# A two-model transformer block on one core: shared SBUF tiles moved to addresses that are multiples of 128 bytes

## The chip, the core and the metric

The kernel runs on 1 core of a Trainium2 chip, as one launch. The metric is the device time of that launch in microseconds (us), the median of several runs. Names of engines: PE is TensorE (matmul), PEld its weight loads, DVE VectorE, ACT ScalarE, POOL GpSimd, SP the queue that starts most DMAs. SBUF is the on-chip memory; addresses in this document are byte offsets within one of its 128 partitions. A fp32r matmul reads fp32 words in one pass; a plain fp32 matmul is split into several.

## What is computed

The reference is a chain of two models on one sequence of 512 tokens and 1024 features, all in fp32. Cut to what matters here:

```python
# first model, two layers
for layer in range(2):
    x = x + 0.5 * swiglu_ffn(rms_norm(x, ...), w_gu[layer], w_down[layer])   # 1024 -> 2 x 2816 -> 1024
    h = rms_norm(x, ...)
    x = x + (even_mixer if layer == 0 else odd_mixer)(h, ...)                # banded, stick-breaking, dilated attention
    x = x + memory_cross_attention(rms_norm(x, ...), rms_norm(mem, ...), ...)# 256 memory rows, 4 heads of 256
    x = x + 0.5 * swiglu_ffn(rms_norm(x, ...), ...)
# second model, one layer
proj = rms_norm(x, ...) @ w_in
y_a = (rg_lru(conv(xr), ...) * gelu(gr)) @ w_rnn_out
y_b = dsa_sparse_attention(q, k, v, iq, ik, iw) @ w_att_out                  # top 128 of the keys per query
mix = (sigmoid(g_a) * y_a + sigmoid(g_b) * y_b) @ w_o
x = x + rms_norm(mix, ...)
f = (silu(h @ w_gate) * (h @ w_up)) @ w_down
x = x + rms_norm(f, ...)

def swiglu_ffn(x, w_gu, w_down):
    gate, up = split(x @ w_gu, 2)
    return (silu(gate) * up) @ w_down
```

## The kernel before

**Big products.** Nearly all the work is a fixed list of products with weights (`gemm_table`), run one after the other by `pe_products`. Activations stand transposed, features on the partitions: a tile `[128, K, 512]` holds K slices of 128 features by 512 tokens (2048 bytes a slice). Precision comes from splitting: each operand is held as an upper part and a remainder, both of type fp32r, and a product is three matmuls, upper by upper, upper by remainder, remainder by upper. The loop runs over column groups of the weight; in a group over chunks of two K slices; over the slice; over up to four output banks; and over the three products. With K slices and four banks a group has K x 4 x 3 matmuls: 96 where K is 8, 264 where K is 22.

**Two forms.** In form A the weights are the stationary operand (128 x 128) and the activations stream past (moving operand, 512 columns). In form B it is the other way round: the activations are stationary, the weights move. In the names of the profile, `ps<-hTh,wh` is written moving operand first.

**Weights.** The SP queue brings weight chunks from HBM into four buffers `raw`; ACT copies each to `wh` (upper part), DVE computes `wl = raw - wh`. Four buffers each, prepared up to three chunks ahead (`act_split`, `dve_split`).

**Activations.** Five kinds of tiles feed the big products:
- `hTh`, `hTl`: the normalised input of most products, with an SBUF place of their own;
- `f..Fh`, `f..Fl` (class `Ffn`): the gated product of a feed-forward, 22 slices, read by the down projection; four times in form A (`f1d0`, `f2d0`, `f1d1`, `f2d1`), the last time in form B (`f3d`);
- `c0mh`, `c0ml` (class `Cross`, and `c1..`): the normalised memory, read by the key and value projection of the cross attention, form B, 4 groups of 48 matmuls per layer;
- `s_Yh`, `s_Yl`: the recurrence's output, form A, 2 groups (within `ya`);
- `s_Zh`, `s_Zl`: the merged branches, form A, 2 groups (`wo`).

**Where tiles lie.** The weights' buffers, `xT` and `hTh`/`hTl` have fixed places below `base`. All other tiles share the space above it and are laid out anew for each stage, by class `Area`: a running offset `at`, and `take`, which gives a tile the offset and steps on by its size rounded up to 32 bytes (lines 148 to 161). `sb` without an area allocates from the fixed part, in the order of the calls (lines 271 to 290). `base` is the end of the fixed part rounded up to 64 (line 296). Small tiles taken in between (one column of 4 bytes, 8 statistics) move what follows by 32 bytes.

```python
    def take(self, nc, name, shape, dt):
        n = 4 * int(np.prod(shape[1:]))
        t = nc.alloc_sbuf_tensor_at(name, shape, dt, offset=self.at)
        self.at += -(-n // 32) * 32
        return t
```

**Attention.** Scores, transposes and value products of the three attention stages are plain fp32 matmuls on tiles of those areas (`o_kT`, `s_kT`, `e_kbT`, `..PT`), mixed by `pe_stage` with the matmuls of the neighbouring big products. The order of everything is written out by hand; there is no scheduler.

**Start.** `x_rows` (the input), `prm` (parameters) and `misc` (identity matrix, masks) are loaded, PE transposes the input, ACT and DVE split it into `hTh` and `hTl`. At the end PE runs `f3d`, then ACT, POOL and DVE scale by the norm and SP stores.

Of the kernel before, what the change touches and what calls it, by code (L numbers as in the profile page):

```python
# [13 lines left out]
P = 128  # L14
# [133 lines left out]
class Area:  # L148
# [4 lines left out]

    def take(self, nc, name, shape, dt):
        n = 4 * int(np.prod(shape[1:]))
        t = nc.alloc_sbuf_tensor_at(name, shape, dt, offset=self.at)
        self.at += -(-n // 32) * 32
        return t
# [13 lines left out]
def params_layout():  # L172
    names = []
    for l in range(2):
        names += [(f"ffn1_norm{l}", 8), (f"mix_norm{l}", 8), (f"xa_norm{l}", 8), (f"xa_mem_norm{l}", 8),
                  (f"ffn2_norm{l}", 8), (f"xa_q_gain{l}", 2), (f"xa_k_gain{l}", 2)]
    names += [("ev_q_gain", 1), ("ev_k_gain", 1), ("od_q_gain", 1), ("od_k_gain", 1), ("ev_sinks", 8),
              ("norm_mix_pre", 8), ("norm_mix_post", 8), ("norm_ffn_pre", 8), ("conv_b", 8), ("rg_b_a", 8), ("rg_b_x", 8),
              ("rg_lambda", 8), ("conv_w", 32)]
    at, off = {}, 0  # L180
    for n, w in names:
        at[n] = (off, w)
        off += w
    return at, off


PRM, NPRM = params_layout()
# [71 lines left out]
def program(nc, T, out):  # L259
    ctx = ExitStack()  # L260

    def sb(name, shape, dt=F32, area=None):
        if area is None:
            return ctx.enter_context(nc.sbuf_tensor(name, shape, dt))
        return area.take(nc, name, shape, dt)
# [12 lines left out]
    wl = [sb(f"wl{i}", [P, 2, 512], F32R) for i in range(NW)]  # L278
    xn_at = nc.sbuf_base
    xn = [sb(f"xn{i}", [P, D]) for i in range(2)]  # L280
    prm = sb("prm", [P, NPRM])
    misc = sb("misc", [P, NMISC])
    half = sb("half", [P, 64])
    stat = sb("stat", [P, 16])
    ones = sb("ones", [P, P])
    rc = sb("rc", [P, 8])
    coef = sb("coef", [P, 8])
    la = sb("la", [P, 5, 8])
# [4 lines left out]
    def rate(t):  # L293
        return rc[:, 4 + t:5 + t]

    base = -(-nc.sbuf_base // 64) * 64

    def par(name):
        o, w = PRM[name]
# [1163 lines left out]
    ev = Area(base)  # L1463
# [10 lines left out]
    ev_gone = ev.sub()  # L1474
    e_ta = sb("e_ta", [P, NT, 512], F32, ev)
    e_kd = sb("e_kd", [P, NT, 256], F32, ev)
    ev.at += 64
    e_R = sb("e_R", [P, S], F32, ev)
    ev_xn = Area(xn_at)
    ev_q = Area(xn_at + 2048)  # L1480
# [1268 lines left out]
```

How the kernel before makes its waits and increments, by code:

```python
    def wait_ge(self, flag, key):  # L75
        if self.e is None:
            return
        sem, value, who, place = flag.at[key]
        if who is not None:
            if self.seen.get(who, 0) >= place:
                return
            self.seen[who] = place
        else:
            if self.seen.get(sem, 0) >= value:
                return
            self.seen[sem] = value
        self.e.wait_ge(sem, value)
# [272 lines left out]
    def handover(e, key):  # L360
        e.last.also(ended, (key, e.name)) if e.last.place else e.last.then_inc(ended, (key, e.name))
        if e.name != "pe":
            for who in ("pe", "act", "dve", "pool"):
                e.wait_ge(ended, (key, who))
# [2 lines left out]
    def sp_weights(sp):  # L368
        for n, (segs, kp) in enumerate(stream):
            r, o = n % NRAW, 0
            if n >= NRAW:
                sp.wait_ge(w_hi, n - NRAW)
                sp.wait_ge(w_lo, n - NRAW)
            for w, c, width, _, _ in segs:
                sp.dma_start(raw[r][:, :, o:o + width], w[kp * 256:(kp + 1) * 256, c:c + width].rearrange(
                    "(c p) n -> p c n", p=P)).then_inc(raw_in[r], n, 16)
                o += width
# [1 line left out]
    def act_split(act, upto):  # L379
        while act.split <= min(upto, len(stream) - 1):
            n = act.split
            W = chunk(n)
            act.wait_ge(raw_in[n % NRAW], n)
            if n >= NW:
                act.wait_ge(w_used, n - NW)
            act.activation(wh[n % NW][:, :, 0:W], raw[n % NRAW][:, :, 0:W], AF.Copy).then_inc(w_hi, n)
```

## Time and profile before

| | us |
|---|---|
| median of 3 runs | 3221.99 (3221.38 to 3222.6) |
| the profiled execution, its own time | 3222.08 |
| its span, first to last instruction | 3220.4 |
| PE busy | 3143.0 (98% of the span) |
| DVE busy | 1573.0 (49%) |
| ACT busy | 1223.4 (38%) |
| POOL busy | 345.3 (11%) |
| HBM traffic | 286.42 MB read, 90 GB/s over the span |

The span and the profiled execution's own time differ by 1.7 us, which lies outside the instructions. Busy is the union of an engine's instructions; a matmul of the trace begins when the one before it is still draining, so for the rate of PE one reads the distance between the starts of two matmuls (below: the interval), not the duration of one (about 0.39 us here). The mean granted TensorE clock is 0.991 of full speed.

### The profile page before, as it was taken

To read this page: it belongs to the slowest core of one execution; us is meant where nothing else is said; L and a number is where in the kernel's file an instruction comes from. 1 tells how busy PE (TensorE), PEld (TensorE's weight loads), DVE (VectorE), ACT (ScalarE), POOL (GpSimd) and SP (SyncE) were. 2 spreads that over 40 slices of the span, in tenths; PEclk is the share of its full clock that TensorE was granted. 3 is DMA by queue.
4 is the path that set the end of the run, shared out by engine and by line. 5 is a ranking of instruction groups with operands and counts; after the bars stand their busy time and mean duration, and the time that the engine had idled before them with its cause. 6 is when DMAs were issued, how large, how long until landed. Compare 5 with 4: busy or idle time off the path is not lost.

```text
span 3220.4 us, 36941 instructions
## 1 busy us (share of the span) xinstructions
PE 3143.0 (98%) x14404; PEld 2517.4 (78%) x14404; DVE 1573.0 (49%) x2425; ACT 1223.4 (38%) x2008; POOL 345.3 (11%) x532
## 2 busy tenths in 40 slices
PE   7999999999999999999999999999999999989998
PEld 6888886777888888888867878888886776768887
DVE  4443347655444344433465554443246876454432
ACT  4232337543332233223465433232336637333221
POOL 1000123211000010001411201000242100010000
PEclk9999999999999999999999999999999999989999
DMA  4332331322333323323322412332322231223331
GB/s 133 100 98 93 98 97 35 121 82 79 98 92 99 98 92 98 99 98 92 87 97 85 138 49 92 102 95 95 89 85 80 70 101 34 85 67 97 99 98 66
DMA packets 212463, 290.93 MB, mean 90 GB/s; under 512 B 12832, under 2 KB 136992, under 8 KB 212160
## 3 DMA queue, kind: packets, MB, share of 16 engines
q1 hardware_dynamic: 209792, 279.59, 27.7%
q0 software_dynamic: 2496, 8.98, 0.9%
q8 instruction: 113, 1.85, 0.2%
q14 instruction: 62, 0.51, 0.0%
HBM read 286.42 MB, written 2.10 MB: 90 GB/s over the span
## 4 chain that ended last, share of the span: by engine, by line
PE 89%; ACT 4%; DVE 3%; POOL 3%; issue 1%; DMA 0%; SPq 0%; POOLq 0%; DVEq 0%; ACTq 0%
PE ps L94 86%; PE ps L97 3%; ACT wh L100 1%; POOL xn L103 0%; POOL evQ L142 0%; ACT L100 0%; DVE wl L103 0%; ACT sxPb L100 0%; ACT ocPb L100 0%; DVE hTl L109 0%; DVE s_ri L115 0%; POOL s_ri L103 0%; ACT xn L100 0%; POOL evPb L142 0%; DMA raw<-in_ffn_w_gu 0%
## 5 line engine op out<-in xcount | busy, mean ns | idle before, releaser
L103 DVE TENSOR_TENSOR wl<-raw,wh 128x1024 fp32r<-128x1024 f32 (+1 forms) x530 | 649.1, 1234 | 1113.1 <-ACT wh L100 1108.2
L100 ACT ACTIVATE wh<-raw 128x1024 fp32r<-128x1024 f32 (+1 forms) x530 | 550.6, 1049 | 1182.5 <-PE ps L94 1111.5
L94 PE MATMUL ps<-hTh,wh 128*128 128x512 f32 x2400 | 948.8, 395 | 24.2 <-DVE wl L103 16.5
L94 PE MATMUL ps<-hTl,wh 128*128 128x512 f32 x2400 | 939.8, 392 | 0.0
L94 PE MATMUL ps<-hTh,wl 128*128 128x512 f32 x2400 | 939.0, 391 | 0.0
L94 PEld LDWEIGHTS ps<-hTh,wh 128*128 128x128 f32 x2400 | 452.5, 189 | 133.5 <-issue 18.9
L94 PEld LDWEIGHTS ps<-hTl,wh 128*128 128x128 f32 x2400 | 452.7, 189 | 97.1 <-issue 6.4
L94 PEld LDWEIGHTS ps<-hTh,wl 128*128 128x128 f32 x2400 | 452.5, 189 | 95.7 <-issue 2.5
L103 POOL TENSOR_TENSOR xn<-xn 128x512 f32<-128x512 f32 x68 | 99.5, 1463 | 1828.4 <-ACT xn L100 1580.2
L94 PE MATMUL ps<-wh,hTh 128*128 128x512 f32 (+2 forms) x576 | 218.4, 379 | 0.9 <-DVE s_ikT L121 0.9
L94 PE MATMUL ps<-wh,hTl 128*128 128x512 f32 (+2 forms) x576 | 216.3, 376 | 0.0
L94 PE MATMUL ps<-wl,hTh 128*128 128x512 f32 (+2 forms) x576 | 215.8, 375 | 0.0
L94 PEld LDWEIGHTS ps<-wh,hTh 128*128 128x128 f32 x576 | 108.9, 189 | 21.6 <-issue 3.7
L94 PEld LDWEIGHTS ps<-wh,hTl 128*128 128x128 f32 x576 | 108.8, 189 | 20.6 <-issue 2.2
L94 PEld LDWEIGHTS ps<-wl,hTh 128*128 128x128 f32 x576 | 108.9, 189 | 19.4 <-issue 1.6
L109 DVE SCALAR_TENSOR_TENSOR hTl<-xT,prm,hTh 128x512 fp32r<-128x512 f32 x72 | 73.7, 1039 | 15.3 <-ACT hTh L100 14.2
L100 ACT ACTIVATE hTh<-xT,prm 128x512 fp32r<-128x512 f32 x72 | 51.2, 716 | 70.0 <-DVE xT L109 40.6
L94 PE MATMUL ps<-wh,f3Fh 128*128 128x512 f32 x176 | 69.7, 396 | 0.0
L94 PE MATMUL ps<-wh,f3Fl 128*128 128x512 f32 x176 | 69.4, 394 | 0.0
L94 PE MATMUL ps<-wl,f3Fh 128*128 128x512 f32 x176 | 69.4, 394 | 0.0
L94 PE MATMUL ps<-f10Fh,wh 128*128 128x512 f32 x176 | 69.3, 394 | 0.0
L94 PE MATMUL ps<-f20Fh,wh 128*128 128x512 f32 x176 | 69.3, 394 | 0.0
(405 smaller groups left out, 4094.7 us busy)
## 6 DMA issues: line engine op xcount, KB each, us to landing
raw<-in_ffn_w_gu SPq DMA_DIRECT2D x352, 256.0 KB, 3.1
raw<-in_ffn_w_down SPq DMA_DIRECT2D x88, 512.0 KB, 3.5
raw<-in_xa_w_kv SPq DMA_DIRECT2D x32, 512.0 KB, 4.0
raw<-in_w_in SPq DMA_DIRECT2D x28, 512.0 KB, 3.7
raw<-in_od_w_in SPq DMA_DIRECT2D x24, 512.0 KB, 3.7
raw<-in_w_ffn_gate SPq DMA_DIRECT2D x44, 256.0 KB, 2.9
raw<-in_w_ffn_up SPq DMA_DIRECT2D x44, 256.0 KB, 3.1
raw<-in_w_ffn_down SPq DMA_DIRECT2D x22, 512.0 KB, 3.9
```

The costliest lines, as they stand in the source:

```text
L94: return self.made(lambda e: e.matmul(*a, **k))
L97: return self.made(lambda e: e.transpose(*a, **k))
L100: return self.made(lambda e: e.activation(*a, **k))
L103: return self.made(lambda e: e.tensor_tensor(*a, **k))
L109: return self.made(lambda e: e.scalar_tensor_tensor(*a, **k))
```

## The change

`Area.take` rounds the offset up to 128 for tiles of 512 bytes per partition or more; `base` is rounded to 128; `ones` and `prm` swap places in the fixed part so that `ones` (512 bytes) begins at such a multiple too; and a skip of 64 bytes ahead of `e_R` becomes 192, so that tiles that lie over each other in the even mixer still do so as before.

```diff
     def take(self, nc, name, shape, dt):
         n = 4 * int(np.prod(shape[1:]))
+        if n >= 512:
+            self.at = -(-self.at // 128) * 128
         t = nc.alloc_sbuf_tensor_at(name, shape, dt, offset=self.at)
         self.at += -(-n // 32) * 32
         return t
...
-    prm = sb("prm", [P, NPRM])
     misc = sb("misc", [P, NMISC])
     half = sb("half", [P, 64])
+    ones = sb("ones", [P, P])
+    prm = sb("prm", [P, NPRM])
     stat = sb("stat", [P, 16])
-    ones = sb("ones", [P, P])
...
-    base = -(-nc.sbuf_base // 64) * 64
+    base = -(-nc.sbuf_base // 128) * 128
...
     e_kd = sb("e_kd", [P, NT, 256], F32, ev)
-    ev.at += 64
+    ev.at += 192
```

No instruction is added, removed or moved: engine by engine the two built programs have the same rows in the same order (13122 merged rows on PE, 2223 on DVE, 1723 on ACT, 351 on POOL, 581 on SP), line numbers aside. Only addresses differ. Those of the built programs, with the remainder on division by 128:

```
tile                      before          after
hTh, hTl            32896, 49280     the same      0, 0   ->  0, 0
raw, wh, wl        65664..114815     the same           0 ->  0
f..Fh               126656           126720            64 ->  0
f..Fl               171712           171776            64 ->  0
f..sg, pr, R        216768..         216832..          64 ->  0
c.mh, c.ml          126656, 134848   126720, 134912    64 ->  0
s_Yh, s_Yl          165792, 182176   165888, 182272    32 ->  0
s_Zh                182176           182272            32 ->  0
s_Zl                130752           130816            64 ->  0
o_qT, o_kT          159712, 176096   159872, 176256    96 ->  0
s_qT, s_kT          130752, 147136   130816, 147200    64 ->  0
e_qbT, e_kbT        155520, 163712   155776, 163968     0 ->  0
evPT, ocPT, sxPT    (three stages)                     64, 96, 32 -> 0
x_rows              126656           126720            64 ->  0
misc                123776           123008             0 ->  0
ones                125888           125056            64 ->  0
```

All slices within the tiles of the big products begin at multiples of 512 bytes from the tile's start, so a tile's remainder is that of every operand taken from it.

## Rows read from the trace of the kernel before

**Rows 1.** The page's first part: the span, and busy time of each engine.
```profile
span 3220.4 us, 36941 instructions
...
PE 3143.0 (98%) x14404; PEld 2517.4 (78%) x14404; DVE 1573.0 (49%) x2425; ACT 1223.4 (38%) x2008; POOL 345.3 (11%) x532
```
**Rows 2.** The page's fourth part: the chain that ended last, by engine and line.
```profile
PE 89%; ACT 4%; DVE 3%; POOL 3%; issue 1%; DMA 0%; SPq 0%; POOLq 0%; DVEq 0%; ACTq 0%
PE ps L94 86%; PE ps L97 3%; ACT wh L100 1%; POOL xn L103 0%; POOL evQ L142 0%; ACT L100 0%; DVE wl L103 0%; ACT sxPb L100 0%; ACT ocPb L100 0%; DVE hTl L109 0%; DVE s_ri L115 0%; POOL s_ri L103 0%; ACT xn L100 0%; POOL evPb L142 0%; DMA raw<-in_ffn_w_gu 0%
```
**Rows 3.** Timeline, PE, first gate and up product: start us, duration us, what.
```profile
72.84 0.39 PE L94 MATMUL ps<-hTh,wh 128*128 128x512 f32 x1
...
246.92 0.39 PE L94 MATMUL ps<-hTh,wh 128*128 128x512 f32 x1
```
**Rows 4.** Timeline, PE, first down projection, and the first matmul after it.
```profile
268.68 0.40 PE L94 MATMUL ps<-f10Fh,wh 128*128 128x512 f32 x1
...
389.55 0.40 PE L94 MATMUL ps<-wh,hTh 128*128 128x512 f32 x1
```
**Rows 5.** Timeline, PE, first matmul of the memory's projection.
```profile
608.51 0.40 PE L94 MATMUL ps<-wh,c0mh 128*128 128x512 f32 x1
```
**Rows 6.** Timeline, PE: second group on Y, its first; wo, its first and what follows.
```profile
2596.85 0.40 PE L94 MATMUL ps<-s_Yh,wh 128*128 128x512 f32 x1
...
2774.15 0.40 PE L94 MATMUL ps<-s_Zh,wh 128*128 128x512 f32 x1
...
2818.95 0.50 PE L94 MATMUL ps<-ones,xn 128*128 128x1 f32 x4
```
**Rows 7.** Timeline, PE, second group of the last down projection: first and last.
```profile
3149.38 0.39 PE L94 MATMUL ps<-wh,f3Fh 128*128 128x512 f32 x1
...
3210.75 0.40 PE L94 MATMUL ps<-wh,f3Fl 128*128 128x512 f32 x1
```
**Rows 8.** Windows: length, then PE, PEld, DVE, ACT, POOL busy (count), clock, DMA.
```profile
72.84:246.92 174.08, 174.08 (x770) 144.19 (x768) 81.05 (x97) 53.05 (x65) 0.00 (x0) 1.00 0.31 97
268.68:389.55 120.87, 120.87 (x530) 99.16 (x528) 40.50 (x40) 32.73 (x38) 7.32 (x6) 1.00 0.28 92
608.51:619.71 11.20, 11.20 (x49) 9.02 (x48) 11.00 (x9) 10.89 (x17) 6.47 (x4) 1.00 0.42 140
2596.85:2619.12 22.27, 22.27 (x96) 17.73 (x95) 21.75 (x50) 3.78 (x5) 0.00 (x0) 1.00 0.40 114
2774.15:2818.95 44.80, 44.80 (x194) 36.06 (x193) 21.29 (x25) 14.02 (x18) 7.55 (x5) 1.00 0.32 102
3149.38:3210.75 61.37, 61.37 (x265) 49.18 (x263) 14.75 (x14) 12.38 (x20) 3.73 (x9) 1.00 0.13 44
```
**Rows 9.** Groups of PE by shape: plain fp32 scores of the three attention stages.
```profile
L94 PE MATMUL ps<-o_kT,o_qT 64*128 64x512 f32 x32 | 9.0, 641 | 0.0
L94 PE MATMUL ps<-s_kT,s_qT 64*128 64x512 f32 x32 | 9.0, 641 | 0.0
...
L94 PE MATMUL ps<-e_kbT,e_qbT 64*128 64x512 f32 x16 | 4.5, 641 | 0.0
```
**Rows 10.** Groups of DVE, ACT and POOL: the same shapes at different remainders.
```profile
L109 DVE SCALAR_TENSOR_TENSOR xT<-ps,xT 128x512 f32<-128x512 f32 x64 | 43.5, 688 | 39.4 <-PE ps L94 39.4
...
L103 DVE TENSOR_TENSOR f10Fl<-f10pr,f10Fh 128x512 fp32r<-128x512 f32 x22 | 14.2, 690 | 1.8 <-ACT f10Fh L100 1.8
...
L100 ACT ACTIVATE f10Fh<-f10pr 128x512 fp32r<-128x512 f32 x22 | 13.6, 633 | 18.0 <-DVE f10pr L103 18.0
...
L100 ACT ACTIVATE s_Yh<-xn 128x512 fp32r<-128x512 f32 x8 | 5.1, 633 | 32.4 <-DVE xn L103 32.4
...
L103 POOL TENSOR_TENSOR xn<-xn 128x512 f32<-128x512 f32 x68 | 99.5, 1463 | 1828.4 <-ACT xn L100 1580.2 <-PE ps L94 245.0
...
L103 POOL TENSOR_TENSOR s_ri<-s_ra 128x512 f32<-128x512 f32 x8 | 9.6, 1204 | 9.7 <-ACT s_ra L100 9.4
```
**Rows 11.** Timeline, PE, the input's transposes at the start, and what released them.
```profile
7.16 5.25 PE L97 MATMUL ps<-misc,x_rows 128*128 128x128 f32 x32 [7.16 <-DMA misc<-in_misc]
```

## The prediction

> **What bounds the kernel now.** I read the page's busy times first: PE works in 98% of the span, twice as much as the next engine [rows 1]. The chain of work that ended last says the same from the other side: 89% of it is PE, 86% the matmuls of line 94 [rows 2]. So time can be won or lost here almost only by what PE does per matmul, and a nanosecond more or less on the common matmul counts thousands of times. Waits are not the subject: in a long product PE never stands idle.
>
> The change moves no instruction; it only moves addresses. So the question is whether the trace of before holds the same work on tiles at different addresses. It does. I took the timeline of PE, looked at the start of the first and of the last matmul of a product, and divided by the number of intervals between. That number is the second count in the windows (weight loads, one per matmul) [rows 8]:
>
> - `hTh`/`hTl`, remainder 0: from 72.84 to 246.92, 174.08 us over 768 matmuls, 226.7 ns each [rows 3, 8].
> - `f10Fh`/`f10Fl`, remainder 64, as moving operand: 120.87 us over 528, 228.9 ns [rows 4, 8].
> - `c0mh`/`c0ml`, remainder 64, as stationary operand: 11.20 us over 48, 233.3 ns [rows 5, 8].
> - `s_Zh`/`s_Zl`, remainders 32 and 64, moving: 44.80 us over 192 (the next product begins at 2818.95; the window counts its weight load as the 193rd), 233.3 ns [rows 6, 8].
> - `s_Yh`/`s_Yl`, remainder 32, moving: 22.27 us over 95, 234.4 ns [rows 6, 8].
> - `f3Fh`/`f3Fl`, remainder 64, stationary: 61.37 us over 263, 233.4 ns [rows 7, 8].
>
> In all six stretches PE is busy for their whole length and the granted clock is 1.00, so the 2.4 GHz level throughout: neither a wait nor the clock makes the difference [rows 8]. Nor does traffic: the last stretch has the lowest DMA share (0.13) and one of the longest intervals, and the fast one has 0.31. Every product whose two operands both have remainder 0 runs at 226.7, every other one is longer. That is the whole case for a gain.
>
> **The change part by part.** The sum is made against the profiled execution, 3222.08 us, whose span is 3220.4; it lies 0.09 above the median of the runs, which is nothing. The gain of a product is its number of matmuls times what its interval exceeds 226.67 ns.
>
> 1. Four down projections in form A, 528 matmuls each. One takes 120.87 us [rows 4]; at the fast interval it would take 528 x 0.22667 = 119.68, so 1.19 each, **4.8 us** together.
> 2. The last down projection, form B, 528 matmuls at 233.35: 528 x 6.68 ns = **3.5 us** [rows 7].
> 3. The memory's projections, 4 groups of 48 per layer, two layers, 384 matmuls at 233.3: 384 x 6.66 ns = **2.6 us** [rows 5].
> 4. `wo`, 192 matmuls: 44.80 - 43.52 = **1.3 us** [rows 6].
> 5. The two groups on Y, 192 matmuls. The measured group has 7.7 ns over the fast interval, and I take only the 6.7 of `wo`, the same form with the same kind of tile, since the rest may be the gates' matmuls and side work there: **1.3 us** [rows 6].
>
> Sum 13.4 us, and all of it on the path, since these stretches are PE and nothing else [rows 8]. Weight chunks must then arrive 1 to 3% sooner, for which there is room: in the down projection ACT is busy 32.7 of 120.9 us, DVE 40.5 and the DMA engines 0.28 of the time [rows 8]. In the first group of the memory's projection DVE is busy 11.0 of 11.2 us and ACT 10.9 [rows 5, 8]; there the cover is thin, and the 0.3 us of that group, twice, may go into a wait for `wl` instead.
>
> The other moved tiles I cost at nothing. Attention scores are plain fp32 matmuls, and the same shape on `o_kT` (remainder 96), `s_kT` (64) and `e_kbT` (0) takes 641 ns in all three stages [rows 9]. DVE and ACT: 690 ns with all operands at 64 against 688 at 0 and in PSUM; 633 ns for ACT from 64 to 64 and from 0 to 32 alike. POOL, which holds 3% of the chain [rows 2], takes 1463 ns for two inputs at 0 and 1204 for the same shape at 64, so it isn't slower off the multiple of 128 [rows 10]. So no vector work becomes shorter; an upper bound from the 2 ns of that DVE pair on some 250 such operations is 0.5 us, off PE's path. `ones` is an operand in 10 norms or so, fractions of a microsecond either way. At the start PE's first transposes wait for `misc`, which is on a multiple of 128 before and after [rows 11]; how a DMA into `x_rows` takes the move the trace doesn't show, and since those transfers overlap the wait of 7.16 us I bound it at 1 us both ways.
>
> A rule of the Trainium skill speaks against all this. The page "SBUF — State Buffer", section "Specifications (TRN2)", gives SBUF lines of 16 bytes; every tile of before begins at a multiple of 32 bytes, so by that rule alone no operand is worse placed than another and the change is worth 0. The measured intervals do not agree with reading it so: 226.7 against 233.3 ns on the same shape.
>
> **The rivals.**
>
> *Nothing changes (3222).* The slow tiles all lie above address 126656 and the fast ones all below 114816, so remainder and region go together in this trace. If the region, or something else of these products, makes the interval, moving them by 64 or 96 bytes does nothing. Against it: `f10Fh` and `s_Zh`/`s_Zl` lie in the same region, in the same form and with the same weights buffers, and have 228.9 and 233.3 ns [rows 4, 6]; what separates them is 64 against 32. The Trainium skill's line of 16 bytes, on the page named above, would end here too. 11 in 100.
>
> *Only one role gains.* If only the stationary side profits, items 2 and 3 remain, 6.1 us: 3216.0. If only the moving side does, items 1, 4 and 5, 7.4 us: 3214.7. For it: at the same remainder of 64 the stationary tiles cost 6.7 ns and the moving ones 2.2 [rows 4, 7], so it may be two mechanisms. 12 in 100.
>
> *Slower: the distance between the two operands.* In the fast products both operands have the remainder 128 on division by 512 (32896, 82048), not only 0 by 128. After the change F, c and Z tiles have 256 or 0 by 512, and the weights still 128. If what makes 226.7 is that the two streams begin at the same place of a 512-byte stretch, the change doesn't restore it. Price: the four down projections, today the mildest case, would take on the interval of the others, 2112 x (233.33 - 228.92) ns = 9.3 us, the rest unchanged: 3231.4. It decides against the change as soon as the interval in the first down projection is above 228.9. Against it: `f10Fh` and `f3Fh` have the same distance from the weights, 64 by 512, and yet 228.9 and 233.4 ns, so the distance alone doesn't set the interval [rows 4, 7, 8]. 5 in 100.
>
> *More than that.* The matmuls of `hTh` that are mixed with attention, and the first dozen after each stall, may settle faster when their neighbours are aligned too, and a remainder of 0 by 256 may be better than 128. Below 3206; 3 in 100.
>
> **How the numbers follow.** The forecast, full gain, has 69 in 100: 3222.1 - 13.4 = **3208.7 us**, its own range 3206 to 3210.5 from the thin cover in item 3 (+0.6), the start (1 both ways) and item 5. What this kernel's runs can tell from no change is about 0.2%, 6.4 us, so the line is 3215.6. Faster by more: 69 + 3 + the half of the one-role case that lies below 3215.6, 6, is 78. Within 0.2%: 11 + 6 = 17. Slower: 5. The range takes in full gain and both one-role cases, 81 in 100: 3206 to 3217.
>
> **What the profile after would show.** Right: the first down projection takes 119.7 us from its first matmul to the next product's first, the groups of 48 take 10.9, `wo` 43.5, the last group of `f3d` 59.6 over 263 intervals, all with PE busy throughout and clock 1.00; `hTh` products, attention, DVE and ACT durations stay to the nanosecond; the last store comes 13 us sooner. Wrong: if the f tiles stay at 228.9 and Z at 233.3 it was not the remainder; if they differ from before but don't reach 226.7, the remainder by 128 is only part of the rule; if they reach it and the end doesn't move by their sum, a wait for `wl` or for a bias has taken it up.

## The result, and the profile after

The changed kernel takes **3230.94 us** (median of 8 runs, 3230.08 to 3231.92); the kernel before, on the same chip, 3221.89 (8 runs, 3220.03 to 3223.33). The ratio is 1.0029, 95% interval 1.0019 to 1.0038: slower by 9 us, where 13 us of gain were forecast. The profiled execution took 3231.92 us with a span of 3230.2.

The page of the changed kernel, busy time of each engine:

```profile
span 3230.2 us, 36941 instructions
...
PE 3152.1 (98%) x14404; PEld 2520.0 (78%) x14404; DVE 1573.1 (49%) x2425; ACT 1224.2 (38%) x2008; POOL 346.4 (11%) x532
```

Against [rows 1] PE is busy 9.1 us longer, and every other engine about as long as before. The chain is what it was: 86% is line 94 on PE, as in [rows 2]. So the time is again in what one matmul costs. The timeline of PE, at the same matmuls as in [rows 3 to 7] (start us, duration us, what):

```profile
74.12 0.39 PE L94 MATMUL ps<-hTh,wh 128*128 128x512 f32 x1
...
248.20 0.39 PE L94 MATMUL ps<-hTh,wh 128*128 128x512 f32 x1
...
269.96 0.40 PE L94 MATMUL ps<-f10Fh,wh 128*128 128x512 f32 x1
...
393.15 0.39 PE L94 MATMUL ps<-wh,hTh 128*128 128x512 f32 x1
...
611.95 0.40 PE L94 MATMUL ps<-wh,c0mh 128*128 128x512 f32 x1
...
623.10 0.40 PE L94 MATMUL ps<-wh,c0mh 128*128 128x512 f32 x1
```

And the windows between such starts (length, then busy time and count of PE, PEld, DVE, ACT, POOL, the clock, DMA share, GB/s):

```profile
74.12:248.20 174.08, 174.08 (x769) 144.19 (x768) 81.05 (x97) 53.11 (x65) 0.00 (x0) 1.00 0.31 97
269.96:393.15 123.19, 123.19 (x529) 99.10 (x528) 40.50 (x40) 32.76 (x38) 7.38 (x6) 1.00 0.28 90
611.95:623.10 11.15, 11.15 (x49) 9.04 (x48) 10.95 (x9) 10.84 (x17) 6.42 (x4) 1.00 0.43 141
2607.50:2629.76 22.26, 22.26 (x96) 17.78 (x95) 21.75 (x50) 3.79 (x5) 0.00 (x0) 1.00 0.39 112
2784.85:2829.64 44.79, 44.79 (x193) 36.04 (x192) 21.29 (x25) 14.02 (x18) 7.56 (x5) 1.00 0.32 102
3159.44:3220.54 61.10, 61.10 (x264) 49.55 (x263) 14.70 (x14) 12.40 (x20) 3.75 (x9) 1.00 0.13 45
```

Read them beside [rows 8], one by one:

| product | before, ns per interval | after | matmuls | worth, us |
|---|---|---|---|---|
| `hT` (addresses unchanged) | 226.7 | 226.7 | | 0 |
| four down projections, form A | 228.9 | **233.3** | 2112 | **+9.3** |
| last down projection, form B | 233.3 | 232.3 | 528 | -0.5 |
| memory, form B | 233.3 | 232.3 | 384 | -0.4 |
| Y | 234.4 | 234.3 | 192 | 0 |
| `wo` | 233.3 | 233.3 | 192 | 0 |

The first down projection alone went from 120.87 to 123.19 us, 2.32 us, with the clock at 1.00 and PE busy for the whole window in both; the trace shows the other three within 0.01 us of it. The sum is +8.4 us. The medians differ by 9.05. The two profiled executions differ by 9.84, of which 1.28 lie ahead of the first window already (74.12 against 72.84). That is scatter of the start: in two runs below, whose start is the kernel before's to the byte, the same matmul begins at 72.46 and at 73.83. Without it 8.56 remain. That this is the sum to 0.2 us is in part luck, since other stretches of the trace moved as well and nearly cancel: +1.06 us between the first layer's memory products and the next down projection, -1.69 ahead of the first matmul on Y, and +1.14 from the first to the last matmul on Y (66.79 against 67.93 us). In that last stretch PE waits for `wl`:

```profile
2580.03 0.50 PE L94 MATMUL ps<-s_Yh,wh 128*128 128x512 f32 x1 [1.24 <-DVE wl L103]
```

Before, the same wait left PE idle for 0.05 us. It does not come from the addresses on Y: run e2 below has them as before and takes 67.94 us there. What moved the other two stretches is not shown.

### The profile page after: what moved, and what is told of

It is laid out like the page before. It is cut to its first block, busy times and chain, and to the rows that moved or that the text cites. A ratio compares the mean times of both kernels' runs of the same rounds, so it can differ in the third digit from the quotient of the medians.

```text
span 3230.2 us, 36941 instructions
## 1 busy us (share of the span) xinstructions
PE 3152.1 (98%) x14404; PEld 2520.0 (78%) x14404; DVE 1573.1 (49%) x2425; ACT 1224.2 (38%) x2008; POOL 346.4 (11%) x532
## 4 chain that ended last, share of the span: by engine, by line
PE 88%; ACT 4%; DVE 3%; POOL 3%; issue 1%; DMA 0%; SPq 0%; POOLq 0%; DVEq 0%; ACTq 0%
PE ps L94 86%; PE ps L97 3%; ACT wh L100 1%; POOL xn L103 0%; ACT L100 0%; POOL evQ L142 0%; DVE wl L103 0%; ACT ocPb L100 0%; ACT sxPb L100 0%; DVE hTl L109 0%; ACT xn L100 0%; DVE s_ri L115 0%; POOL s_ri L103 0%; POOL evPb L142 0%; DMA raw<-in_ffn_w_gu 0%
## 5 line engine op out<-in xcount | busy, mean ns | idle before, releaser
L94 PE MATMUL ps<-f10Fh,wl 128*128 128x512 f32 x176 | 69.5, 395 | 0.0
L94 PE MATMUL ps<-f20Fh,wl 128*128 128x512 f32 x176 | 69.5, 395 | 0.0
L94 PE MATMUL ps<-f11Fh,wl 128*128 128x512 f32 x176 | 69.5, 395 | 0.0
L94 PE MATMUL ps<-f21Fh,wl 128*128 128x512 f32 x176 | 69.5, 395 | 0.0
```

Of the source, the lines that this page charges most:

```text
L94: return self.made(lambda e: e.matmul(*a, **k))
```

## The experiments

Two theories come out of this. **Distance**: what counts is the difference between the address of the activations and that of the weights, not the remainder of either. Before the change the down projections had +64 bytes (192 against 128 by 512), now +128; `hT` has 0. **Place**: it is the address itself or the region, and 128 by 512 is a good place while 256 is a bad one. Beside them stands the period, 512 or less.

In what follows a helper table gives each feed-forward's tiles an address of their own (`f20Fh` and `f20Fl` are those of the product `f2d0`, and so on), and the distance is activation minus weights, in bytes, until it is said otherwise.

**e1, e2: a sweep of the distance.** From the kernel before, e1 with the distances `f1d0` 0, `f2d0` 256, `f1d1` 128, `f2d1` 32, `f3d` 0, and e2 with -32, -64, 192, 96, 256:

```diff
+FF_AT = {'f10': 128, 'f20': 384, 'f11': 256, 'f21': 160, 'f3': 128}
...
-            area = Area(base)
+            area = Area(base + (FF_AT[tag] - base) % 512)
```

> The kernel before, but each of the five feed-forwards gets its own place: remainders by 512 of f10, f20, f11, f21, f3 are 128, 384, 256, 160, 128; the weights' buffers stay at 128. Distance from the weights: 0, 256, 128, 32, 0. Theory 'distance' (an interval of 226.7 ns needs both operands of a matmul at the same place of a 512 or 256 byte stretch): f1d0 and f3d run at 226.7, f1d1 repeats the 233.3 of the changed kernel, f2d0 is 226.7 if the period is 256 and over 228 if it is 512, f2d1 is over 228. Theory 'region' (tiles above address 126656 are slow wherever they begin): no product reaches 226.7, f1d0 and f3d stay at 228.9 and 232 to 234.

> As the first sweep, with distances -32, -64, 192, 96 in form A (f10, f20, f11, f21) and 256 in form B (f3). Theory 'distance': none in form A is at 226.7; the values between 228 and 234 give the shape of the dependence, and if it is symmetric then -64 is at the 228.9 that +64 had before. f3d at 256 tells whether form B has a period of 256 (226.7) or 512 (about 232 to 234). Theory 'region': all between 228.9 and 233.4 in no order.

Timeline of PE in e1, `f2d0` and `f1d1`, each from its first matmul to the first of the next product:

```profile
1026.44 0.39 PE L95 MATMUL ps<-f20Fh,wh 128*128 128x512 f32 x1
...
1146.12 0.39 PE L95 MATMUL ps<-hTh,wh 128*128 128x512 f32 x1
...
1387.34 0.40 PE L95 MATMUL ps<-f11Fh,wh 128*128 128x512 f32 x1
...
1510.53 0.39 PE L95 MATMUL ps<-wh,hTh 128*128 128x512 f32 x1
```

At a distance of 256 the 528 matmuls take 119.68 us, 226.67 ns each, as they do at 0 (`f1d0`, 268.65 to 388.33). At 128 they take 123.19 us, just what the changed kernel has. 32 gives 233.34. In e2 -32, -64, 192 and 96 all give 233.3 to 233.4, and the last product, form B at 256, has the fast interval (59.62 us over 263, 226.7 ns):

```profile
3158.16 0.39 PE L95 MATMUL ps<-wh,f3Fh 128*128 128x512 f32 x1
...
3217.78 0.39 PE L95 MATMUL ps<-wh,f3Fl 128*128 128x512 f32 x1
```

e1 took 3220.31 us and e2 3229.35, one run each (before: 3221.49). So the period is 256, not 512, and a remainder of 0 by 128 of both operands is not enough: `f1d1` in e1 has it and takes 233.3 ns. But the weights stand at 128 by 512 in all of these, so distance and place are not yet apart.

**e3: the weights moved.** 64 bytes ahead of the weights' buffers put `wh` and `wl` at 192 by 512; `hT` stays at 128, and the feed-forwards get the distances 0, -64, 256, +64 and 0:

```diff
+FF_AT = {'f10': 192, 'f20': 128, 'f11': 448, 'f21': 256, 'f3': 192}
...
+    gap = sb("gap", [P, 16])
     wh = [sb(f"wh{i}", [P, 2, 512], F32R) for i in range(NW)]
```

> The kernel before with 64 bytes left free ahead of the weights' buffers wh and wl, so that they have the remainder 192 by 512, while hTh and hTl stay at 128 and raw too. Feed-forwards at 192, 128, 256, 256, 192 (f10, f20, f11, f21, f3): distances 0, -64, 64, 64, 0. Theory 'distance': f1d0 and f3d at 226.7; all products on hTh/hTl, at distance -64, leave 226.7 and take 228.9 to 233.4, some 8600 matmuls of 512 columns, so 19 to 58 us longer in all, less some 5 us. Theory 'place of the activation tile' (its own remainder of 128 is what counts): hTh/hTl stay at 226.7, f2d0 reaches it, f1d0 and f3d don't, time 3215 to 3222. Theory 'remainder 128 of both': nothing reaches 226.7 but nothing of hTh/hTl can keep it either, f1d0 included; that is told from 'distance' by f1d0 and f3d alone.

Timeline of PE in e3, `f2d0` and `f1d1`:

```profile
1042.51 0.39 PE L95 MATMUL ps<-f20Fh,wh 128*128 128x512 f32 x1
...
1165.71 0.39 PE L95 MATMUL ps<-hTh,wh 128*128 128x512 f32 x1
...
1413.85 0.40 PE L95 MATMUL ps<-f11Fh,wh 128*128 128x512 f32 x1
...
1533.55 0.39 PE L95 MATMUL ps<-wh,hTh 128*128 128x512 f32 x1
```

`f2d0` now lies at the "good" place, 128 by 512, and takes 123.20 us (233.3 ns); `f1d1` lies at 448, no multiple of 128, and takes 119.70 (226.7). The products of `hTh` in form A, whose own tiles have not moved a byte, went from 226.8 to 233.3 ns, and the kernel to 3262.01 us. Place and region fall; distance stands. The run also explains the milder case: form A at +64 (`f2d1`) has 228.9 ns again, at -64 233.3; form B, the products of `hT` in `in1` and `qkv`, where the weights are now the moving operand and lie 64 ahead, has 229.1. So what is mild is that the **moving** operand is 64 bytes ahead of the stationary one; the other sign is not.

One product of this run doesn't fit. `s_Zh` and `s_Zl` move along with the weights here (182240 and 130816), so that `wo` has the distances +32 and +64, as before. Yet its 192 matmuls take 44.14 us over 191 intervals, 231.1 ns, where they had 233.3:

```profile
2811.49 0.39 PE L95 MATMUL ps<-s_Zh,wh 128*128 128x512 f32 x1
...
2855.63 0.40 PE L95 MATMUL ps<-s_Zh,wl 128*128 128x512 f32 x1
```

So where the two parts of the activations have different distances, the distance to the weights alone doesn't fix the interval. Y, with +32 in both parts, stays at 233.2.

**e4: distance 0 everywhere.** From the kernel before, F, c, Y and Z moved to 128 by 512, nothing else:

```diff
+            area = Area(base + (FF_AT[tag] - base) % 512)
...
-            st = Area(base)
+            st = Area(base + (128 - base) % 512)
...
-    a0, a1 = base, sp_area.at
+    a0, a1 = base, sp_area.at + (128 - sp_area.at) % 512
...
```

> The kernel before with only the tiles of the big products moved: F, c, Y and Z tiles all begin at a remainder of 128 by 512, like hTh, hTl and the weights; everything else keeps to the layout of before, not rounded. Theory 'distance': all intervals 226.7, the sum of the prediction is then due, 13.4 us: 3208.5 (3207 to 3210). Theory 'place': the same. Theory 'region': 3222. If only one role of the operand depends on it: 3214 to 3216.

It took 3210.15 us (5 runs, 3208.91 to 3211.95), ratio to before 0.9964, interval 0.995 to 0.9978: faster than both kernels.

**e7: one part of the change undone.** From the changed kernel, with only the feed-forward tiles back at their old addresses:

```diff
+    near = 128
+
     def take(self, nc, name, shape, dt):
...
-            self.at = -(-self.at // 128) * 128
+            self.at = -(-self.at // self.near) * self.near
...
-            area = Area(base)
+            area = Area(base - 64)
+            area.near = 64
```

> The changed kernel with one part undone: the feed-forward tiles (f..Fh, f..Fl, sg, pr, R) lie again at 126656 and so on, exactly where they were before the change, a distance of 64 bytes ahead of the weights by 256; all other tiles stay where the change put them. Theory 'distance by 256' (the interval of a matmul hangs on activation address minus weight address, modulo 256): the four form A down projections return from 233.32 to 228.9 ns, the last one (form B) from 232.4 to 233.3, memory, Y and Z products stay as after the change. Time 3230.9 - 9.3 + 0.5 = 3222.1 us, within 0.1% of the kernel before. Rival 'the slowdown sits elsewhere' (in base, ones, prm, the attention tiles or the start, while the intervals only go along): stays near 3231.

3221.4 us (10 runs), ratio to before 0.9999, interval 0.999 to 1.0009. The first down projection is back at 120.87 us:

```profile
268.78 0.40 PE L94 MATMUL ps<-f10Fh,wh 128*128 128x512 f32 x1
...
389.65 0.40 PE L94 MATMUL ps<-wh,hTh 128*128 128x512 f32 x1
```

The whole slowdown hangs on where the feed-forward tiles lie, and the rest of the change (`base` for the other stages, `ones`, `prm`, the attention tiles) is worth nothing that these runs can tell (the interval leaves room for 0.1%, 3 us). The trace agrees: from the first matmul on `hTh` on, no stretch between the products is more than 0.2 us from that of before.

**e8: the change with another remainder.** From the changed kernel, one line, so that F, c and `s_Zl` lie 256 bytes from the weights' remainder, Y and `s_Zh` at 0, by 512:

```diff
-    base = -(-nc.sbuf_base // 128) * 128
+    base = nc.sbuf_base + (128 - nc.sbuf_base) % 256
```

> The changed kernel with one line different: base is the end of the fixed part rounded up not to a multiple of 128 but to the next address that leaves 128 on division by 256 (126848), so that F, c, Y and Z tiles all lie at 384 or 128 by 512 while the weights are at 128 by 512. Theory 'distance by 256': every big product runs at 226.7 ns (memory and Y 227.2 to 227.5), 3208.5 to 3210.5 us, like the earlier run with only F, c, Y and Z at 128 by 512, and about 21 us below the changed kernel. Rival 'distance by 512': Y runs fast, F, c and Z (256 away) stay near 233.3, 3229 us. Rival 'other tiles matter too': a time below 3208, since attention and vector tiles are moved as well.

3209.69 us (5 runs, 3209.38 to 3210.6), ratio to before 0.9965, interval 0.9953 to 0.9978, about 21 us below the changed kernel. Its page and the timeline of its first down projection, first memory group and last product:

```profile
PE 3128.0 (98%) x14404; PEld 2516.1 (78%) x14404; DVE 1574.0 (49%) x2425; ACT 1223.3 (38%) x2008; POOL 344.6 (11%) x532
```

```profile
268.55 0.39 PE L94 MATMUL ps<-f10Fh,wh 128*128 128x512 f32 x1
...
388.23 0.39 PE L94 MATMUL ps<-wh,hTh 128*128 128x512 f32 x1
...
608.31 0.39 PE L94 MATMUL ps<-wh,c0mh 128*128 128x512 f32 x1
...
619.19 0.39 PE L94 MATMUL ps<-wh,c0mh 128*128 128x512 f32 x1
...
3138.66 0.39 PE L94 MATMUL ps<-wh,f3Fh 128*128 128x512 f32 x1
...
3198.28 0.39 PE L94 MATMUL ps<-wh,f3Fl 128*128 128x512 f32 x1
```

119.68 us for the down projection, 10.88 for the memory group, 59.62 over 263 intervals for the last product: each is the size that the prediction gave it. Neither a period of 512 nor an effect of other tiles is left: e4, where the attention tiles, `ones` and `prm` keep their old addresses, takes 3210.15 us, and from the first matmul on `hTh` on each stretch between the products is within 0.1 us of e8's.

A part of the gain goes into waits all the same. The second memory group waits longer for `wl` than before, and so does Y (before, then twice e8; from the timeline of PE, the idle time in brackets):

```profile
626.53 0.50 PE L94 MATMUL ps<-wh,c0mh 128*128 128x512 f32 x1 [1.06 <-DVE wl L103]
...
626.31 0.50 PE L94 MATMUL ps<-wh,c0mh 128*128 128x512 f32 x1 [1.52 <-DVE wl L103]
...
2562.74 0.50 PE L94 MATMUL ps<-s_Yh,wh 128*128 128x512 f32 x1 [1.72 <-DVE wl L103]
```

From first to last matmul the memory products take 47.30 us in e8 against 47.91 in the first layer, 0.6 us less where the intervals are worth 1.3; and the stretch of Y takes 67.73 against 66.79, 0.9 us more, though the interval within it fell from 233.4 to about 227 ns.

**e6: the gaps in the sweep.** From the kernel before, distances 320, 160, 288, 64, and -64 in form B:

```diff
+FF_AT = {'f10': 448, 'f20': 288, 'f11': 416, 'f21': 192, 'f3': 64}
```

> From the kernel before: each feed-forward's tiles at a place of their own, all else as before; activation minus weight address: f1d0 +320, f2d0 +160, f1d1 +288, f2d1 +64 (as before), f3d (form B) -64. Theory 'distance by 256, and a milder case where the moving operand is 64 ahead': f1d0 (320 is 64 by 256, moving operand ahead) 228.9 ns, f2d0 (160) 233.3, f1d1 (288 is 32 by 256) 233.3, f2d1 228.9, f3d (moving weights 64 ahead of the stationary activations) 229.1 instead of the 233.3 of before. Rival 'period 512': f1d0 and f1d1 differ from what 64 and 32 gave. Time near 3221.5 + 4.66 + 4.66 ns x 528 - 4.2 ns x 528 = 3224 us.

Timeline of PE in e6, `f1d0` and the second group of `f3d`:

```profile
268.30 0.40 PE L95 MATMUL ps<-f10Fh,wh 128*128 128x512 f32 x1
...
389.17 0.40 PE L95 MATMUL ps<-wh,hTh 128*128 128x512 f32 x1
...
3152.25 0.39 PE L95 MATMUL ps<-wh,f3Fh 128*128 128x512 f32 x1
...
3212.45 0.40 PE L95 MATMUL ps<-wh,f3Fl 128*128 128x512 f32 x1
```

320 gives 120.87 us, as 64 did; 288 gives 233.3 ns, as 32 did. The last product, with its moving weights now 64 ahead, falls from 61.37 us [rows 7, 8] to 60.20, 228.9 ns per interval. The sign rule holds in both forms. 160 was a miss by a little: 123.69 us, 234.3 ns, the longest of all. Time 3223.92 us, one run.

**e5, e9: the two parts at different distances.** e5, from the kernel before, has 128 bytes between `wh` and `wl`, so that `wl` lies at 256 by 512, and Fh, Fl at chosen places; e9 leaves the weights alone and only separates Fh from Fl.

```diff
+    gap = sb("gap", [P, 32])
     wl = [sb(f"wl{i}", [P, 2, 512], F32R) for i in range(NW)]
...
+            hi = sb(tag + "Fh", [P, KF, S], F32R, area)
+            area.at += (at_lo - area.at) % 512
+            self.F = Act(hi, sb(tag + "Fl", [P, KF, S], F32R, area), S, ("F", up))
```

> From the kernel before: 128 bytes of room between the weights' upper parts (wh, 128 by 512) and remainders (wl, now 256 by 512), and Fh, Fl of each feed-forward at addresses of their own. The three matmuls of a step are: weights upper with Ah, weights upper with Al, weights lower with Ah. Theory NEXT: the stream of the moving operand meets the load of the following matmul's stationary operand, so the distance that counts is moving operand of one matmul against stationary operand of the next. Theory OWN: the distance between the two operands of the same matmul counts. By (Fh, Fl) modulo 256, mean intervals in ns: f1d0 (128, 128) both 228.9, but OWN has the third matmul of each three slow and NEXT the second; f2d0 (128, 0) NEXT 226.7, OWN 231.1; f1d1 (0, 128) NEXT 233.3, OWN 228.9; f2d1 (0, 0) both 231.1; f3d in form B (128, 0) NEXT 226.9, OWN 231.1. The products of hTh and hTl get slower by about 2.2 ns each in both (some 8,600 matmuls, so the whole kernel near 3240 us).

> From the kernel before: only Fh and Fl of each feed-forward at places of their own; weights (upper and lower alike) and all else as before. Distances from the weights by 256, as (Fh, Fl): f1d0 (0, 128), f2d0 (128, 0), f1d1 (0, 64), f2d1 (64, 0), f3d (0, 128), form B. Of the three matmuls of a step two read Fh and one reads Fl. Theory 'each matmul by itself': a step costs the sum of its matmuls, so f1d0 226.7 + 6.65/3 = 228.9 ns, f2d0 226.7 + 2 x 6.65/3 = 231.1, f1d1 226.7 + 2.25/3 = 227.4, f2d1 228.2, f3d 226.9 + 5.5/3 = 228.7. Rival 'each change of distance between neighbours costs too', for which the run with weights' parts 128 apart speaks (a matmul at distance 0 between others was slow there): f1d0 231.1, two slow matmuls for the one with Fl, and f2d0 233.3. Time near 3221.5 us in the first case (0, +1.2, -0.8, -0.4, -2.4 against before: 3219.1), about 3223 in the second.

Mean intervals in ns, all five products:

| run | f1d0 | f2d0 | f1d1 | f2d1 | f3d |
|---|---|---|---|---|---|
| e5 | 231.1 | 231.1 | 228.9 | 233.3 | 231.1 |
| e9 | 228.9 | 228.9 | 232.0 | 233.3 | 231.1 |

Timeline of PE in e9, `f2d0`, Fh at 128 and Fl at 0, where 231.1 or 233.3 was expected; it is 120.86 us, 228.9 ns:

```profile
1028.25 0.40 PE L95 MATMUL ps<-f20Fh,wh 128*128 128x512 f32 x1
...
1149.11 0.40 PE L95 MATMUL ps<-hTh,wh 128*128 128x512 f32 x1
```

Both runs are mostly misses. In e5 neither the distance within a matmul nor that to the next one's stationary operand gives the five values (the first gives three of them, `f2d0`, `f1d1` and `f3d`); `hT` in form A had 231.1 instead of 228.9, which made the kernel 3258.09 us instead of some 3240. In e9 the sum of single matmuls gives `f1d0` and fails on the other four; its time is 3226.37 us (one run each). One regularity is left. Nine of the ten values are 226.67 plus 1, 2 or 3 times 2.22 ns, that is, a step of three matmuls costs 680 ns plus a whole number of delays of 6.67 ns. The exception is 232.0 (`f1d1` in e9, a distance of 64 in Fl alone). Runs with one distance show it too: 228.9 ns is one delay per step, and the records of the first down projection before have it unevenly, 231.7, 225.9 and 229.1 ns on average after the first, second and third matmul of a step; 233.3 is three. Which pairing of the streams makes a delay stays open. For the five feed-forwards, which decide the change, it doesn't matter, since upper and lower parts have the same distance there.

## Why the prediction was wrong

**What bounds the kernel** was right: PE's interval decides, and the matmuls of the feed-forwards explain the difference (+9.3 and -0.5 us of 9.05; undoing their move undoes it, e7). That waits are not the subject holds less well: on Y the one for `wl` grew by 1.2 us in the changed kernel and by 1.7 in e8.

**The failed step** is one sentence: "Every product whose two operands both have remainder 0 runs at 226.7, every other one is longer." It is true of the rows, and was read as the cause; from it item 1 took that the four down projections would run at 226.67 ns after the change, and they ran at 233.3. In the only fast products both operands lay at 128 by 512; the remainder by 128 of each, the remainder by 256 and 512, and a difference of 0 were one and the same there. The runs show that, with both parts at the same distance, the difference modulo 256 is what counts: 226.7 ns at 0 and 256 whatever the remainders (448 and 192 in e3), 233.3 at 128 with both remainders 0.

Point by point:

1. Down projections, -4.8 us forecast: +9.3. They had the mild case of +64 and got +128.
2. Last down projection, -3.5: -0.5. In form B 128 costs 232.3 where -64 cost 233.3.
3. Memory, -2.6: -0.4 by the intervals, for the same reason, and -0.2 from first to last matmuls. The thin cover of DVE and ACT didn't matter in its first group, which takes 10.88 us in e8. It did in the second: there the wait for `wl` grows by 0.46 us in e8, of 1.28 us that the layer was to gain.
4. `wo`, -1.3: 0, one slow distance for another.
5. Y, -1.3: 0 by the interval, but +1.1 us with the wait for `wl`, which the prediction didn't have. It saw a thin cover in item 3 alone, though its rows had one in the second group on Y too, where DVE is busy 21.75 of 22.27 us [rows 8].

With the condition met, in e8, three of the five sizes were right: 1.19 us for each down projection in form A, 3.4 for the last one, 1.3 for `wo`. Memory gave about 1.2 of 2.6 us, and Y lost 0.9 instead of gaining 1.3. That e8 is at 3209.7 where the sum says 3208.7 is therefore partly luck: other stretches became shorter by 2.7 us together, and why is not shown. The zeros were right: `f10Fl` 690 ns on DVE and 634 for ACT against 690 and 633 [rows 10], scores 641 again [rows 9].

**The rivals.** The one called slower named the mechanism, the place, the price (9.3 us) and the result (3231.4); it had 5 in 100. Its only flaw is the period, 256 instead of 512, which makes no difference at a distance of 128. What was held against it, that `f10Fh` and `f3Fh` have the same distance and yet 228.9 and 233.4 ns, compared activation with weights in both; but the roles are exchanged in form B, and counted as moving minus stationary the two are +64 and -64. The case for "only one role gains" rested on the same pair and falls with it. "Nothing changes" falls too: three kernels that differ in addresses alone take 3209.7, 3221.4 and 3230.9 us. So does what the prediction concluded from the 16-byte lines that the Trainium skill gives ("SBUF — State Buffer", "Specifications (TRN2)"), that the addresses here, all multiples of 32 bytes, are worth nothing; of the lines themselves no run here says anything.

What could have been seen beforehand: the address table gave all differences, and as moving minus stationary the trace had 0 (226.7 ns), +64 (228.9), -64 and +32 (233.3): an order that the distance explains and the remainder doesn't, since 64 stands in it with two values. No product at 128 existed in the trace, so its price was an extrapolation, and the text took the favourable end. It bounded the DMA into `x_rows`, which the trace doesn't show either, from both sides; for the moved products the nearest rows, the slow ones at +32 and -64, gave 233.3 as the upper bound.

## What to carry to other kernels

Where matmuls with 512 fp32r columns follow each other without a gap, lay the tiles out so that moving and stationary operand differ by a multiple of 256 bytes, in the upper parts and in the remainders alike; aligning each to 128 does not ensure that, and moving only one of the two can make things worse, as here. Then look for the waits that faster matmuls bring out. Compare the two addresses, counted as moving minus stationary, before ordering by the remainder of each. And when several explanations coincide in the rows, find the quantity in which the changed kernel leaves all rows of before: there the forecast has no support, and its chance should say so.

## What the runs showed of the hardware

The interval of back-to-back 128 x 128 by 512 fp32r matmuls hangs on the distance between its two SBUF operands, at the full clock (1.00 in the windows of before and after). The table has the down projections of all runs, both parts at the same distance, moving minus stationary, modulo 256 (products of `hT`, memory and Y at distance 0 have 226.8 to 227.6):

| distance | form A, ns | form B, ns |
|---|---|---|
| 0 | 226.7 | 226.7 to 226.9 |
| 32 | 233.3 | |
| 64 | 228.9 | 228.9 |
| 96 | 233.4 | |
| 128 | 233.3 | 232.3 |
| 160 | 234.3 | |
| 192 | 233.3 | 233.3 |
| 224 | 233.3 | |

Of these, 0, 32, 64 and 192 were measured with the weights at 128 and at 192 by 512 (32 on Y in e3), the others with 128 alone.

The weight loads themselves don't show it: the mean is 189 ns for those of `hTh` before and 189 in e3, where each interval of the same products is 6.5 ns longer. The matmul's duration shows a part of it: for `f10Fh` with `wh` the mean is 394 ns before, 395 after, 389 in e8. The row of e8, from the trace's groups by shape (count, busy us, mean ns, idle before):

```profile
L94 PE MATMUL ps<-f10Fh,wh 128*128 128x512 f32 x176 | 68.5, 389 | 0.0
```

A possible reading is that the stream of the moving operand and the load of a stationary one get in each other's way, with a period of 256 bytes. It was not shown, and e5, e9 and `wo` in e3 show that the simplest form of it is not enough.
